# Last mixer of a three-layer block: 20 taps of a depthwise convolution's first channel tile on TensorE, and tap rounds and lower halves set anew

## The reference

```python
u = rms_norm(h, mix_norm_g)
proj = u @ w_in                       # 1024 x 2560
q, k, v, glu_a, glu_g = split(proj)   # 512 columns each
attn_out = attention(q, k, v)         # 8 heads of 64, T5 bias, causal within 256 tokens
c = glu_a * sigmoid(glu_g)            # 512 channels
c = depthwise_causal_conv(c, 31 taps) + b
conv_out = silu(layer_norm(c))
h = h + concat(attn_out, conv_out) @ w_out
```

## Time and profile before

| | |
|---|---|
| median of 3 runs | 1931.08 us (1928.7 to 1931.2) |
| the profiled execution's own time | 1929.27 us |
| its span | 1927.2 us |
| busy: TensorE, VectorE, ScalarE, GpSimd | 95%, 71%, 58%, 3% |
| mean granted clock of TensorE | 0.973 |
| the last mixer's projections begin | 1602.83 us |
| the third output unit begins | 1710.68 us |

### The profile page before, as it was taken

One profiled execution on the slowest core, in us unless ns is written; L12 is line 12 of the kernel. 1 busy time (PEld: TensorE's weight loads), 2 busy tenths in 40 slices (PEclk: granted clock), 3 DMA queues, 4 the chain that ended last, 5 costly groups with the idle time before them and its releaser, 6 DMA issues.

```text
span 1927.2 us, 26162 instructions
## 1 busy us (share of the span) xinstructions
PE 1833.9 (95%) x10199; PEld 1564.5 (81%) x10199; DVE 1371.4 (71%) x1217; ACT 1108.7 (58%) x1028; POOL 65.0 (3%) x53
## 2 busy tenths in 40 slices
PE   8998999899889999999999999999999987779998
PEld 7897999788768878888788788887887867769997
DVE  3755545634578888888888888887888877964454
ACT  4543443344447677767676777776767753433433
POOL 0001000100200000000000000000000001120000
PEclk9998999899989999999999999999999998989999
DMA  9824555533549999999899999998999982335551
GB/s 271 292 91 154 175 190 180 175 110 110 165 162 365 342 326 376 336 331 376 311 357 344 330 369 339 335 368 310 367 340 333 369 304 77 110 99 176 187 183 44
DMA packets 252147, 490.47 MB, mean 254 GB/s; under 512 B 14172, under 2 KB 96645, under 8 KB 251710
## 3 DMA queue, kind: packets, MB, share of 16 engines
q1 hardware_dynamic: 248000, 474.67, 70.6%
q0 software_dynamic: 3184, 14.29, 2.1%
q10 hardware_dynamic: 910, 0.76, 0.1%
HBM read 488.61 MB, written 5.80 MB: 257 GB/s over the span
## 4 chain that ended last, share of the span: by engine, by line
PE 88%; DVE 8%; issue 2%; ACT 2%; DMA 0%; DVEq 0%; SPq 0%; ACTq 0%
PE psum L546 26%; PE psum L548 26%; PE psum L549 26%; PE psum L984 2%; PE psum L1056 2%; DVE psum L2035 2%; PE psum L1030 1%; PE psum L634 1%; PE psum L665 1%; DVE wl L1569 1%; ACT wh L1177 1%; DVE u L1969 1%; DVE small L1614 1%; DVE x L1626 0%; DMA ring<-in_w_in_ab 0%
## 5 line engine op out<-in xcount | busy, mean ns | idle before, releaser
L1569 DVE TENSOR_TENSOR wl<-ring,wh 128x2048 fp32r<-128x2048 f32 x443 | 1015.0, 2291 | 355.7 <-ACT wh L1177 355.0
L1177 ACT ACTIVATE wh<-ring 128x2048 fp32r<-128x2048 f32 x450 | 861.6, 1915 | 417.2 <-PE psum L546 348.3
L546 PE MATMUL psum<-wh,xTh 128*128 128x512 f32 (+1 forms) x1136 | 436.3, 384 | 6.4 <-DVE wl L1569 3.8
L549 PE MATMUL psum<-wh,xTl 128*128 128x512 f32 (+1 forms) x1136 | 425.8, 375 | 0.0
L548 PE MATMUL psum<-wl,xTh 128*128 128x512 f32 (+1 forms) x1136 | 425.8, 375 | 0.0
L546 PE MATMUL psum<-xTh,wh 128*128 128x256 f32 x1088 | 313.1, 288 | 6.2 <-ACT gnat L1417 1.9
L548 PE MATMUL psum<-xTl,wh 128*128 128x256 f32 x1088 | 310.1, 285 | 0.0
L549 PE MATMUL psum<-xTh,wl 128*128 128x256 f32 x1088 | 309.9, 285 | 0.0
L546 PE MATMUL psum<-wh,wnh 128*128 128x512 f32 x672 | 266.8, 397 | 0.0
L548 PE MATMUL psum<-wl,wnh 128*128 128x512 f32 x672 | 264.3, 393 | 0.0
L549 PE MATMUL psum<-wh,wnl 128*128 128x512 f32 x672 | 263.8, 393 | 0.0
(11 more groups left out here) (264 smaller groups left out, 1196.6 us busy)
## 6 DMA issues: line engine op xcount, KB each, us to landing
ring<-in_w_moe SPq DMA_DIRECT2D x336, 1024.0 KB, 5.2
ring<-in_w_dense SPq DMA_DIRECT2D x33, 1024.0 KB, 5.2
ring<-in_w_in_ab SPq DMA_DIRECT2D x14, 1024.0 KB, 11.0
ring<-in_w_in_cd SPq DMA_DIRECT2D x12, 1024.0 KB, 5.3
ring<-in_w_gate SPq DMA_DIRECT2D x11, 1024.0 KB, 5.4
ring<-in_w_up SPq DMA_DIRECT2D x11, 1024.0 KB, 5.3
ring<-in_w_down SPq DMA_DIRECT2D x11, 1024.0 KB, 4.9
ring<-in_w_in SPq DMA_DIRECT2D x10, 1024.0 KB, 5.8
```

Source lines behind the costliest of these rows:

```text
L546: last = pe.matmul(o, a[0], b_[0], start=first, stop=False)
L549: return pe.matmul(o, a[1], b_[0], start=False, stop=final)
L1177: act.activation(upper_half[i], ring[:, u_, :], ACT.Copy).then_inc(hi_ready[s_], 1)
L1569: dve.tensor_tensor(lower_half[i], ring[:, u_, :], upper_half[i].bitcast(F32), ALU.subtract)\
```

## The change

TensorE sums the bias and taps 0 to 19 of tile 0 in bank 3, with diagonal matrices of the tap weights as one operand, in f32. GpSimd makes the diagonals, four at a time, in two alternating blocks in `nw`; it begins a block when the taps that used it are summed. The bias now lies in row 0 of `convw`, so tap j has column j + 1 of `cw`. VectorE's first tap of tile 0 is tap 20; it adds to bank 3 and signals `conv_taken`, for which the first values wait, as they write the same bank. The rounds of taps are set anew: 17 of tile 1 alone, 5 of three tiles, 9 of four, 2 of (0,2,3), and (2,3) once in gaps 9, 17 and 18 and twelve times in a new gap 19. Gap 19 stands behind the lower half of the turned heads, which stood behind all taps. `out_unit(1)` goes ahead of the wait for the convolution. GpSimd makes the lower halves 0, 4, 5 and 9 (before: 2, 4, 6); VectorE makes 1, 2, 3, 6, 7, 8 and 10 (before: 0, 1, 3, 5, 7, 8, 9, 10). Upper halves that follow the copy of a finished unit, in all three mixers, wait for nothing more (`copied=True`).

```diff
@@ -96,16 +96,23 @@
 STEPS_GLU = 43
-POOL_LOWERS = (2, 4, 6)
-CONV_MOVED = [30, 30, 20, 20]
-FIRST_TILE = 0
-B2_TAPS = {**{i: [(0, 1)] * 3 for i in range(4)}, **{i: [(0, 1, 2, 3)] * 2 for i in (4, 5, 6, 7, 12, 13)},
-           **{i: [(0, 1, 2, 3), (2, 3)] for i in (8, 9, 10, 11, 14)}, 15: [(2, 3)] * 2, 16: [(2, 3)] * 2, 17: [(2, 3)] * 5}
+POOL_LOWERS = (0, 4, 5, 9)
+PE_TAPS = [2, 4, 2, 4, 2, 2, 2, 2]
+HANDED = sum(PE_TAPS)
+B2_TAPS = {0: [(1,)] * 6, 1: [(1,)] * 5, 2: [(1,)] * 3, 3: [(1,)] * 3, 4: [(1, 2, 3)], 5: [(1, 2, 3)], 6: [(1, 2, 3)] * 2, 7: [(1, 2, 3)],
+           8: [(0, 1, 2, 3)], 9: [(0, 1, 2, 3), (2, 3)], 10: [(0, 1, 2, 3)], 11: [(0, 1, 2, 3)] * 2,
+           **{i: [(0, 1, 2, 3)] for i in (12, 13, 14, 15)}, 16: [(0, 2, 3)], 17: [(0, 2, 3), (2, 3)], 18: [(2, 3)], 19: [(2, 3)] * 12}
+CONV_MOVED = [HANDED + 7, 29, 13, 13]
...
     return [s for s, p in enumerate(places) if p == gap]
...
+def taps_at(gap):
...
+    return range(sum(PE_TAPS[:gap]), sum(PE_TAPS[:gap + 1]))
@@ -1099,14 +1110,29 @@
+            def conv_taps(i):
+                for j in taps_at(i):
+                    if j == 0:
+                        pe.wait_ge(conv_in, 1)
+                        first_of(pe.matmul(bank[3][:, 0:T], convw[0:1, 0:P], cum[0:1, 0, :], start=True, stop=False))
+                    if j % 4 == 0:
+                        pe.wait_ge(diag_ready, j // 4 + 1)
+                    last = pe.matmul(bank[3][:, 0:T], diag[:, j % 8, :], upad[:, 0, j:j + T], start=False, stop=(j == HANDED - 1))
+                    first_of(last)
+                    if j % 4 == 3:
+                        last.then_inc(conv_tapped, 1)
...
             def b2_gap(i):
...
                     trio_scores(B2_FIRST + s)
+                conv_taps(i)
                 if i == B2_OUT_TURNED:
...
                 for s in at(B2_VALUES, i):
+                    if s == 0:
+                        pe.wait_ge(conv_taken, 1)
                     if s == 3:
@@ -1131,6 +1157,7 @@
             turn_out(1, bank[0], 8, B2_FIRST + 6)
+            out_unit(1, 10)
             pe.wait_ge(a_pT, B2_FIRST + 6)
@@ -1138,7 +1165,6 @@
                 last.then_inc(conv_turned, 1)
-            out_unit(1, 10)
             pe.wait_ge(conv_out, 2)
@@ -1165,13 +1191,16 @@
-            def upper(after=None, count=0):
+            def upper(after=None, count=0, copied=False):
...
                     act.wait_ge(after, count)
+                elif copied:
+                    pass
                 elif not isinstance(n, int) or n >= 2:
@@ -1517,18 +1546,14 @@
                     copy_step(nv[:, :, 256 * (w // 9):256 * (w // 9) + 256])
-                if w == 0:
-                    upper(split_used[0], LENGTHS[0] + 1)
-                elif w == 2:
-                    upper(split_used[0], LENGTHS[0] + 3)
-                elif w > 2:
-                    upper()
+                if w != 1:
+                    upper(copied=True)
                 if w >= 2:
...
             b2_gap(17)
+            b2_gap(18)
             upper()
-            b2_gap(18)
             out_upper(1, bank[0], 10)
@@ -2017,7 +2042,7 @@
-            tapped = [0] * 4
+            tapped = [HANDED, 0, 0, 0]
@@ -2029,11 +2054,16 @@
                     tapped[c] += 1
-                    if j == 0:
-                        last = dve.tensor_scalar(summed(c, 0), upad[:, c, 0:T], cw[:, c, 0:1], cw[:, c, 31:32], ALU.mult, ALU.add)
+                    w = cw[:, c, j + 1:j + 2]
+                    if c == 0 and j == HANDED:
+                        dve.wait_ge(conv_tapped, HANDED // 4)
+                        dve.scalar_tensor_tensor(summed(c, j), upad[:, c, j:j + T], w, bank[3][:, 0:T], ALU.mult, ALU.add)\
+                           .then_inc(conv_taken, 1)
+                        dve.wait_ge(conv_taken, 1)
+                    elif j == 0:
+                        last = dve.tensor_scalar(summed(c, 0), upad[:, c, 0:T], w, cw[:, c, 0:1], ALU.mult, ALU.add)
                     else:
-                        last = dve.scalar_tensor_tensor(summed(c, j), upad[:, c, j:j + T], cw[:, c, j:j + 1], summed(c, j - 1),
-                                                        ALU.mult, ALU.add)
+                        last = dve.scalar_tensor_tensor(summed(c, j), upad[:, c, j:j + T], w, summed(c, j - 1), ALU.mult, ALU.add)
                 link(last)
@@ -2051,12 +2081,10 @@
                 if i == 14:
-                    assert all(n > m for n, m in zip(tapped[FIRST_TILE:], CONV_MOVED[FIRST_TILE:]))
+                    assert all(n == m + 1 for n, m in zip(tapped, CONV_MOVED))
                     dve.nop().then_inc(conv_moved, 1)
             glu(0)
-            for _ in range(2):
-                taps(0, 1)
             for w in range(2, 10):
@@ -2066,10 +2094,11 @@
             b2_gap(17)
+            b2_gap(18)
+            out_lower(1, bank[0], 10)
+            b2_gap(19)
             assert tapped == [CONV] * 4
             dve.nop().then_inc(conv_done, 1)
-            b2_gap(18)
-            out_lower(1, bank[0], 10)
             dve.wait_ge(late_in, 80)
@@ -2077,7 +2106,7 @@
                 asked.append(ask_for(t, dve.tensor_scalar(e2[:, t:t + 1], mv[:, 2 * t + 1:2 * t + 2], LN_EPS, None, ALU.add)))
-            lower()
+            halves.skip()
             for t in range(TT):
@@ -2172,7 +2201,15 @@
-            for n in POOL_LOWERS:
+            pool.wait_ge(step_evac, STEPS_GLU - 2)
+            for b in range(HANDED // 4):
+                if b == 2:
+                    lower(1, 0)
+                if b >= 2:
+                    pool.wait_ge(conv_tapped, b - 1)
+                pool.tensor_tensor(diag[:, 4 * (b % 2):4 * (b % 2) + 4, :], ident[:, :].unsqueeze(1).broadcast_to([P, 4, P]),
+                                   cw[:, 0, 4 * b + 1:4 * b + 5].unsqueeze(2).broadcast_to([P, 4, P]), ALU.mult).then_inc(diag_ready, 1)
+            for n in POOL_LOWERS[1:]:
                 lower(1, n)
...
             lower(1, 11)
```

More of the change, by code:

```diff
@@ L354, in build @@
         moe_done = sem("moe_done")
+        diag_ready = sem("tap_diagonals_ready")
+        conv_tapped = sem("four_taps_done")
+        conv_taken = sem("first_channels_taken_over")
         conv_moved = sem("conv_sums_in_sbuf")
@@ L413, in build @@
         upad = gA[:, :, 0:CONV - 1 + T]
+        diag = nw.rearrange("p t n -> p (t n)").rearrange("p (j c) -> p j c", j=8)
         block = ctx.enter_context(nc.Block())
@@ L2162, in _ @@
             pool.wait_ge(late_in, 16)
-            pool.dma_start(convw[0:31, :], conv_w_2[0]).then_inc(late_in, 16)
-            pool.dma_start(convw[31:32, :], conv_b_2).then_inc(late_in, 16)
+            pool.dma_start(convw[1:32, :], conv_w_2[0]).then_inc(late_in, 16)
+            pool.dma_start(convw[0:1, :], conv_b_2).then_inc(late_in, 16)
             pool.dma_start(convg[:, :], conv_ln_g_2.broadcast_to([P, 512])).then_inc(late_in, 16)
```

## The result

The changed kernel takes 1941.87 us, median of 5 runs (1939.07 to 1944.77); the kernel before, on the same chip, 1931.08 (5 runs, 1928.7 to 1932.83). The ratio is 1.0051, interval 1.004 to 1.0062: **slower, by some 10 us** (10.8 between the medians). The forecast was 1938.3 in a range of 1930 to 1942: the median lies inside the range, close to its upper end, and above the 1935.5 to 1941 that the likeliest case was given. The profiled execution took 1939.11 us with a span of 1937.3, against 1929.27 and 1927.2 before: +9.8 in the time and +10.1 in the span, where +8.0 was forecast for this execution.

What follows compares the result with a forecast made beforehand. TensorE is busy nearly all the span, but in the last mixer VectorE's taps carry the chain. Terms -5.6 + 12.4 + 1.2 = +8.0 us on 1929.27 give 1937.3 for the profiled execution; forecast median 1938.3, range 1930 to 1942.

Steps and rivals of the forecast that it cites:

- the likeliest case: Last mixer: GpSimd's lower half 9 holds VectorE's gap-18 tap round; +8.0 us in all, chance 0.50.
- TensorE's taps: Units 0 to 6: bias and twenty taps at 0.22 us each, 4.6, plus 1.4 for changes of kind, 6.0 us.
- V: End of the last values in the last mixer, forecast at 1690.2, 5.6 us earlier than before.
- Stalls that TensorE's work fills: Ahead of unit 6: TensorE's new work fills the 5.3 us it stood still, and the slow clock behind goes.
- Unit 6 to V: From unit 6 to the last values: 42.0 us of work, 3.1 of waits and 1.5 of clock loss.
- The hold: Gap 18: GpSimd's lower half 9 blocks VectorE's (2,3) round over two SBUF tensors; costs 4.1 us.
- V to the third output unit: From last values to third output unit: held round, twelve bare rounds, layer norm; 27.3 us against 14.9, +12.4.
- The cold clock: Third output unit starts with a cold TensorE clock: 1.2 us.
- VectorE stays the bound: Rival: last mixer's stage stays bound by VectorE and is simply shorter; output unit 6.5 us earlier, 1923.7; chance 0.12.
- no hold: Rival: GpSimd's lower half 9 doesn't block VectorE's gap-18 tap; +3.9 us, about 1934.1; chance 0.26.
- TensorE's taps buy nothing: Rival: TensorE's taps only fill gaps, with full losses of clock and no hold; 1935.7; chance 0.02.
- Longer stalls: Rival: GpSimd's tiles or lower halves 4 and 5 late, clock low from 1676 on; +10.7 or above, 1941 up; chance 0.10.

Runs made afterwards that it cites:

- experiment 4: Changed kernel with TensorE leaving out ten of its twenty taps, for measurement only: median 1939.76 us, 1.0034 of the kernel before.
- experiment 3: Kernel before with only `copied=True` for upper halves behind a unit's copy, in all three mixers: median 1932.01 us, 1.0001 of the kernel before.
- experiment 1: Changed kernel with lower half 9 made by VectorE behind its last tap instead of by GpSimd: median 1939.35 us, 1.0037 of the kernel before.
- experiment 2: Changed kernel with `out_unit(1)` back behind the convolution's transposes: median 1941.19 us, 1.0055 of the kernel before.
- experiment 6: Experiment 5 with `out_unit(1)` behind the transposes and lower half 9 by VectorE between statistics and normalization: median 1930.94 us, 0.9999 of the kernel before.
- experiment 7: Experiment 6 with lower half 6 on GpSimd and two more (2,3) rounds in gap 11: median 1929.59 us, 0.9989 of the kernel before.
- experiment 8: Experiment 7 with 16 TensorE taps instead of 20, VectorE taking four more, one (2,3) round moved to gap 19: 1928.15 us, 0.9989 of before.
- experiment 5: Changed kernel with nine of gap 19's twelve (2,3) rounds moved to gaps 5, 7, 12 and 17: median 1937.7 us, 1.0042 of before.

## Why the prediction was right and where it was off

The likeliest case happened, by its mechanism, and larger: +11.9 in the stage for +8.0. In the span of the profiled execution 1.8 of it doesn't show, because unit 0 started 1.14 earlier and the end was 0.67 shorter.

- **TensorE's taps: the step that failed, in size.** "Eight of that shape take 1.89 us, 0.22 apart: 21 x 0.22 = 4.6", and with 1.4 for changes of kind, 6.0. Unit 6 came 43.83 us behind unit 0, and six units of 5.77 are 34.6, so bias and taps cost 9.2. One product of 256 columns in plain f32 shows as two records. The x8 of the earlier trace rows were four products, which line 841 of the kernel before says: two blocks of columns by two tiles of rows in the loop. Four taps show as x8 after, and experiment 4 measured 0.43. Twenty make 8.6 and the bias about 0.6; the changes of kind, put at 1.4, cost nothing that can be seen. The error is 3.1 us at V: earlier by 2.5 instead of 5.6.
- **Stalls that TensorE's work fills.** Right that they go: no wait for a lower half, full clock behind unit 6 (1.00). But it isn't the taps alone that do it: in experiment 4 ten taps are gone, and the lower half for unit 6 still stands at 1642.82, 2.3 us ahead of the unit. VectorE's shorter queue gives it in time. The diagonals took 1.04 us (estimated 1.2) and were hidden; `copied=True` gave 0 in the kernel before (experiment 3).
- **Unit 6 to V.** Forecast 46.6, measured 90.48 - 43.83 = 46.65. The wait for step 27 is 1.96 (forecast 2.0), for the exponentials 0.98 (1.1). Behind them the clock is 0.74 from 1678.46 to 1685.00 with TensorE busy 5.56 us: 5.56 x 0.26 = 1.4 lost (1.5, which was the middle between two bounds: that it came so close is in part luck).
- **The hold.** Right, and shown by experiment 1. Forecast 4.1, on the path 3.3: two taps lost 4.08, of which 0.84 lay in a wait for a copy that was due anyway. The Trainium skill, "SBUF — State Buffer", section "Who interferes with whom", has a GpSimd tensor_tensor exclude a VectorE instruction with two SBUF inputs; 4.95 us beside GpSimd's 4.50, and 0.87 without it, agree.
- **V to the third output unit.** Forecast 27.3, measured 26.77: twelve rounds 10.95 (10.9), then 9.29 from their end at 1709.65 (9.4). The wait ahead of the transposes was to be some 5 us and was 2.91, since `out_unit(1)` took 8.0 us, from 1698.93 on, at a granted clock of 0.69; VectorE's taps ended last all the same.
- **The cold clock.** Forecast 1.2, measured 18.70 - 16.19 = 2.5: the clock of 1710 to 1720 is 0.53 and the unit's first dozen products stand 0.43 apart, as at the lower level, before they come down to 0.23. I had taken a half of such a loss (1.7 and 3.1 in the earlier trace rows); behind three bare waits it was all of it, 12 steps 0.20 longer each. What exactly decides it stays open: in experiment 2, with one long wait and then a unit of work, the third output unit ran at full clock.

So -2.5 + 11.9 + 2.5 = +11.9. The rival "VectorE stays the bound" is out, since VectorE idles up to 3.43 us at a time ahead of V; "no hold" is out by experiment 1; "TensorE's taps buy nothing" is not settled: V did come 2.5 earlier, but no run leaves all taps to VectorE with the other edits in place, and experiments 6, 7 and 8 show how little the whole brings at best. "Longer stalls" named a time that fits, 1941 and up, but not this way: no half was late, and of its three parts only the low clock in the output units came, by 1.3 more than forecast. Where the change's gain went: its own taps cost TensorE 9.2 us where the stalls for lower halves had been 5.3, so that unit 6 starts 43.83 us behind unit 0 in place of 40.29; what V gains comes behind that, 46.65 us in place of 52.68, from a clock that stays up and shorter waits. And the twelve rounds put behind V cost more than all of it, although VectorE had idle time ahead of V for nine of them (experiment 5).

## What to carry to other kernels

Before a product is priced from a group in the trace, count the products that the code issues for that group: a record isn't always one instruction, and here the price was off by a factor of two. Work given to a second engine pays only if the first then finishes earlier at the place where all wait for it; taps put behind the last values stand bare, whatever was saved ahead. And where a lower half moves to GpSimd, look at which VectorE instructions with two SBUF operands fall beside it, not at the sum of either engine's work.

## What the runs showed of the hardware

- A product of 128x256 in plain f32 occupies TensorE for 0.43 us, two records of 0.215, while the weight matmuls of the same shape stand 0.12 apart: more than three times as much. A change between the two kinds costs nothing that can be seen.
- The start of unit 0 varied by 6.0 us (1601.69 to 1607.72) between executions with practically the same work ahead. In five of the ten executions of the table (experiments 1, 3, 4, 6 and 8; 1604.13 to 1607.72) the page gives a granted clock of 8 tenths in the first of its forty slices; in the other five (1601.69 to 1604.74) it gives 9. A difference of 2 us between two single runs thus says nothing here; the table above is free of it. Why the first slice differs is open.
